# Loading the gate-up weights of a mixture of experts in pairs of chunks, ahead of the down weights

## The reference, cut to what matters

```
for each of 32 experts e:                      # every token has 4 of them
    h = xb @ w_gu[e] + b_gu[e]                 # w_gu[e]: 1024 x 2048, 8 MB
    h_gate, h_up = split(h, 2)                 # clipped at 7
    act = h_gate * sigmoid(1.702 * h_gate) * (h_up + 1)
    y[tokens of e] += gate * (act @ w_down[e] + b_down[e])   # w_down[e]: 1024 x 1024, 4 MB
```

## Time and profile before

| what | us |
|---|---|
| median of 3 runs (2065.43 to 2068.64) | 2066.38 |
| the profiled execution: time | 2069.82 |
| its span, first to last instruction | 2068.0 |
| PE busy | 1988.8 |
| DVE busy | 894.7 |
| ACT busy | 686.3 |
| first expert's first gate-up matmul | 1150.93 |

### The profile page before, as it was taken

One profiled execution on the slowest core, in us unless ns is written; L12 is line 12 of the kernel. 1 busy time (PEld: TensorE's weight loads), 2 busy tenths in 40 slices (PEclk: granted clock), 3 DMA queues, 4 the chain that ended last, 5 costly groups with the idle time before them and its releaser, 6 DMA issues.

```text
span 2068.0 us, 29157 instructions
## 1 busy us (share of the span) xinstructions
PE 1988.8 (96%) x12306; PEld 1384.8 (67%) x12306; DVE 894.7 (43%) x1070; ACT 686.3 (33%) x941; POOL 39.1 (2%) x30
## 2 busy tenths in 40 slices
PE   8999999999999998999999999999999999999997
PEld 8998768999999886999998544444343333433343
DVE  6766666676666787666645211111111111111112
ACT  5545475545555566444444111111001000101011
POOL 0700000000000000000000000000000000000000
PEclk9999999999999998999999899999999999999999
DMA  9663607556556442555296999999999999999997
GB/s 317 196 223 131 235 1 257 191 184 200 170 190 208 166 162 74 173 202 184 95 333 247 372 426 427 427 428 428 429 428 429 428 429 428 429 428 429 428 429 318
DMA packets 165568, 603.88 MB, mean 292 GB/s; under 512 B 9324, under 2 KB 102464, under 8 KB 140564
## 3 DMA queue, kind: packets, MB, share of 16 engines
q1 hardware_dynamic: 165328, 602.79, 74.9%
q10 hardware_dynamic: 164, 0.04, 0.0%
HBM read 601.71 MB, written 1.09 MB: 291 GB/s over the span
## 4 chain that ended last, share of the span: by engine, by line
PE 69%; DMA 22%; DVE 4%; ACT 3%; issue 1%; SPq 0%; DVEq 0%; ACTq 0%
PE ps L1832 13%; PE ps L1834 13%; PE ps L1833 13%; PE ps L2412 12%; DMA sb_w_free<-in_moe_w_gate_up 7%; PE ps L2436 5%; DMA sb_raw<-in_moe_w_down 5%; DMA sb_raw<-in_moe_w_gate_up 3%; DMA sb_w_free<-in_moe_w_down 3%; PE ps L2382 2%; DMA sb_nat_more<-in_moe_w_gate_up 2%; DMA sb_late_raw<-in_moe_w_down 2%; ACT sb_w_hi L669 1%; PE ps L2444 1%; PE ps L2393 1%; DVE sb_w_lo L1112 1%
## 5 line engine op out<-in xcount | busy, mean ns | idle before, releaser
L1112 DVE TENSOR_TENSOR sb_w_lo<-sb_raw,sb_w_hi 128x2048 fp32r<-128x2048 f32 x175 | 403.0, 2312 | 233.8 <-ACT sb_w_hi L669 233.3
L669 ACT ACTIVATE sb_w_hi<-sb_raw 128x2048 fp32r<-128x2048 f32 x179 | 340.5, 1912 | 167.9 <-PE ps L1834 147.6
L1832 PE MATMUL ps<-sb_xT_hi,sb_w_hi 128*128 128x256 f32 x1344 | 373.2, 278 | 0.0
L1833 PE MATMUL ps<-sb_xT_lo,sb_w_hi 128*128 128x256 f32 x1344 | 372.7, 277 | 0.0
L1834 PE MATMUL ps<-sb_xT_hi,sb_w_lo 128*128 128x256 f32 x1344 | 372.6, 277 | 0.0
L1833 PEld LDWEIGHTS ps<-sb_xT_lo,sb_w_hi 128*128 128x128 f32 x1344 | 252.8, 188 | 1.5
L1832 PEld LDWEIGHTS ps<-sb_xT_hi,sb_w_hi 128*128 128x128 f32 x1344 | 252.3, 188 | 1.7 <-DVE sb_w_lo L1112 0.2
L1834 PEld LDWEIGHTS ps<-sb_xT_hi,sb_w_lo 128*128 128x128 f32 x1344 | 253.2, 188 | 0.0
L1027 ACT ACTIVATE sb_h_rows<-ps 128x512 f32<-128x512 f32 x32 | 19.2, 599 | 424.1 <-PE ps L2412 424.1
L1707 DVE COPY sb_h_rows<-ps 128x512 f32<-128x512 f32 x31 | 21.4, 692 | 317.2 <-PE ps L2412 317.2
L1834 PE MATMUL ps<-sb_w_hi,sb_a_lo 128*128 128x512 f32 x352 | 138.5, 393 | 0.0
(11 more groups left out here) (320 smaller groups left out, 2678.8 us busy)
## 6 DMA issues: line engine op xcount, KB each, us to landing
sb_raw<-in_moe_w_gate_up SPq DMA_DIRECT2D x49, 2048.0 KB, 34.5
sb_w_free<-in_moe_w_gate_up SPq DMA_DIRECT2D x46, 2048.0 KB, 34.5
sb_w_free<-in_moe_w_down SPq DMA_DIRECT2D x24, 2048.0 KB, 33.9
sb_raw<-in_ffn_w_up SPq DMA_DIRECT2D x44, 1024.0 KB, 5.3
sb_raw<-in_ffn_w_down SPq DMA_DIRECT2D x44, 1024.0 KB, 5.0
sb_raw<-in_moe_w_down SPq DMA_DIRECT2D x22, 2048.0 KB, 33.9
sb_raw<-in_ffn_w_gate SPq DMA_DIRECT2D x43, 1024.0 KB, 5.4
sb_late_raw<-in_moe_w_gate_up SPq DMA_DIRECT2D x17, 2048.0 KB, 35.2
```

Of the source, the lines that this page charges most:

```text
L669: sc.activation(w_hi[:, c % CUT, :], raw[:, c % RAW, :], ACT.Copy).then_inc(hi_made, 1)
L1112: ve.tensor_tensor(w_lo[:, c % CUT, :], raw[:, c % RAW, :], w_hi[:, c % CUT, :].bitcast(F32), ALU.subtract).then_inc(lo_made, 1)
L1832: pe.matmul(o, l_hi, r_hi, start=start, stop=False)
L1833: pe.matmul(o, l_hi, r_lo, start=False, stop=False)
```

## The change

Places 4 and 5 become adjacent in SBUF: `raw` and `w_free` are now parts of one tensor, `ring_space`. The order of a step's chunks becomes gate-up 0, gate-up 1, down 0, down 1, gate-up 2, gate-up 3, in the loads and on PE, and so for all steps. In steps 5 to 29 (gate-up of experts 6 to 30) two gate-up chunks whose places are adjacent (0 and 1, 4 and 5, 6 and 7) are one DMA of 4 MB, in which a partition gets 32 KB in one piece. It waits until both places are free and signals the semaphore of the first place; PE waits for it before the first chunk of the pair and for nothing before the second. A pair that would lie in places 2 and 3 stays two DMAs (`alone`). Since a partition now holds four neighbouring rows of a pair, a chunk that is loaded alone reads 16 KB of each 32 KB, and `gather` takes every fourth column of x where it took every second. The numbers of the kept down chunks and of the chunk after which outputs are read move by one.

```
-        raw = sb("raw", [P, RAW, CH])
         cuts = ExitStack()
+        sb("below_cuts", [P, RAW, CH], stack=cuts)
...
-        w_free = sb("w_free", [P, 2 * CUT, CH])
+        ring_space = sb("ring_space", [P, RAW + 2 * CUT, CH])
+        raw, w_free = ring_space[:, 0:RAW, :], ring_space[:, RAW:RAW + 2 * CUT, :]
...
+        slot_pairs = {k: ring_space[:, 4 * k:4 * k + 4, :].rearrange("p a n -> p (a n)") for k in range(3)}
+        pair_at = {0: 0, 4: 1, 6: 2}
...
+        def alone(t, first):
+
+            start, end = step_t(LOOP_S[0]) if first else 4, step_t(N_E - 2)
+            return t % 2 == 0 or t % RING == 3 or t < start or t >= end or (t - 4) % EXPERT_C in (2, 3)
...
-                    src = a["moe_w_gate_up_2"][0][bass.ds(e, 1), 256 * j:256 * (j + 1), :].rearrange(
-                        "e (p k) n -> p (e k) n", p=P)
+                    src = a["moe_w_gate_up_2"][0][bass.ds(e, 1), 512 * (j // 2):512 * (j // 2 + 1), :].rearrange(
+                        "e (p q k) n -> p q (e k) n", p=P, q=2)[:, j % 2]
...
+            def gate_up_pair(e, j, t, laps=0):
+
+                if alone(t + 1, isinstance(laps, int)):
+                    expert_chunk("gate_up", e, j, t, laps)
+                    expert_chunk("gate_up", e, j + 1, t + 1, laps)
+                    return
+                src = a["moe_w_gate_up_2"][0][bass.ds(e, 1), 256 * j:256 * (j + 2), :].rearrange("e (p k) n -> p (e k n)", p=P)
+                sp.wait_ge(chunk_used, used_no(t + 1, laps) - RING)
+                sp.dma_start(slot_pairs[pair_at[t % RING]], src).then_inc(slot_loaded[t % RING], 16)
...
             def step_loads(e, s, laps=0, first=0):
 
+                t = step_t(s)
                 if first == 0:
-                    expert_chunk("gate_up", e + 1, 0, step_t(s), laps)
+                    gate_up_pair(e + 1, 0, t, laps)
                     for j in range(2):
-                        if step_t(s) + 1 + j not in KEPT_T:
-                            expert_chunk("down", e, j, step_t(s) + 1 + j, laps)
-                for j in range(max(1, first), 4):
-                    expert_chunk("gate_up", e + 1, j, step_t(s) + 2 + j, laps)
+                        if t + 2 + j not in KEPT_T:
+                            expert_chunk("down", e, j, t + 2 + j, laps)
+                gate_up_pair(e + 1, 2, t + 4, laps)
...
-                    j, odd = divmod(k0 + m, 2)
-                    w = slice(2 * j * P + odd, 2 * (j + 1) * P, 2)
+                    j, row = divmod(k0 + m, 4)
+                    w = slice(4 * j * P + row, 4 * (j + 1) * P, 4)
...
-                pe.wait_ge(slot_loaded[t % RING], loaded_no(t, laps, r))
+                if alone(t, isinstance(r, int)):
+                    pe.wait_ge(slot_loaded[t % RING], loaded_no(t, laps, r))
...
-                gate_up_rows(left, t, 0, laps, r)
+                for j in range(2):
+                    gate_up_rows(left, t + j, j, laps, r)
                 pe.wait_ge(m_g_made, e + 1)
                 turn_picks(base4, s)
                 pe.wait_ge(m_act_made, e + 1)
                 for j in range(2):
-                    down_rows(t + 1 + j, j, laps, r)
+                    down_rows(t + 2 + j, j, laps, r)
...
-                for j in range(1, 4):
+                for j in range(2, 4):
                     gate_up_rows(left, t + 2 + j, j, laps, r)
```

More of the change, by code:

```diff
@@ L94 @@
 LOOPS = (N_E - 8) // 4
-KEPT_T = (4 + EXPERT_C * KEPT_E + 1, 4 + EXPERT_C * KEPT_E + 2)
+KEPT_T = (4 + EXPERT_C * KEPT_E + 2, 4 + EXPERT_C * KEPT_E + 3)
 REL_W = 256
@@ L327, in build, with loaded_no @@
         used_no = lambda t, laps: MOE_C0 + t + 1 + RING * laps
[L329 to L333, removed]
+        def alone(t, first):
+            start, end = step_t(LOOP_S[0]) if first else 4, step_t(N_E - 2)
+            return t % 2 == 0 or t % RING == 3 or t < start or t >= end or (t - 4) % EXPERT_C in (2, 3)
+        def loaded_no(t, quads, r):
+            own = lambda first: [k for k in range(t % RING, ROUND_C, RING) if alone(k, first) and k not in KEPT_T]
+            upto = lambda first: len([k for k in own(first) if k <= t])
+            in_quad = 16 * (3 if t % 2 == 0 or t % RING == 3 else 1) * quads
+            if isinstance(r, int):
+                return 16 * upto(True) + in_quad
+            return 16 * (upto(False) + len(own(True)) - len(own(False))) + in_quad + 16 * len(own(False)) * r
         g_kv, g_in, g_out = (lambda i: 8 * i), (lambda i: 8 * i + 1), (lambda i: 8 * i + 6)
@@ L570, in _ @@
             sp.wait_ge(chunk_used, MOE_C0 - 1)
-            expert_chunk("down", 0, 0, 5)
+            expert_chunk("gate_up", 1, 1, 5)
             sp.wait_ge(chunk_used, MOE_C0)
-            expert_chunk("down", 0, 1, 6)
-            expert_chunk("gate_up", 1, 1, 7)
+            expert_chunk("down", 0, 0, 6)
+            expert_chunk("down", 0, 1, 7)
             sp.wait_ge(logits_done, 1)
@@ L1052, in step @@
                 turned_picks(e, s % 2)
-                outputs(e, s % 2, t + 2, laps)
+                outputs(e, s % 2, t + 3, laps)
             def last_two(r):
@@ L2581, in first_round @@
                     for s in LOOP_S:
-                        step(4 * it, it, s, 3 * it, 0)
+                        step(4 * it, it, s, it, 0)
                 step(0, 0, N_E - 3, 0, 0)
@@ L2589, in another_round @@
                     for s in range(8):
-                        step(N_E * r + 8 * it, QUADS * r + 2 * it, s, 6 * it, r)
+                        step(N_E * r + 8 * it, QUADS * r + 2 * it, s, 2 * it, r)
                 for s in range(N_E - 8, N_E - 2):
```

## The result

The change makes the kernel **slower by 0.5%**: 2077.20 us (median of 6 runs, 2074.02 to 2080.38) against 2066.43 us (6 runs), ratio 1.005 with a 95% interval of 1.0037 to 1.0063. I had forecast 2066.3 us within 2062.8 to 2071.5 us; both the value and the range missed.

A forecast was written before the change was run, and what follows sets the result against it. The weight stream was taken to set the pace from about 1430 us (29.37 us a step), PE before that and in the tail. +3.4 - 3.5 = -0.1 us gave 2066.3 us from 2066.38 us, range 2062.8 to 2071.5 us.

The forecast's parts named there:

- part 4: Order on PE and gather's stride of 4: at worst 0.24 us a step, hidden, so nothing at the end.
- the hole: PE's wait before a paired block in the DMA-paced part: one of about 2.9 us a step in place of three short ones.
- part 3: The ring: a pair waits for its later place, issued some 4 us later; queue 34.5 us deep, never empty, priced at nothing.
- three signs of a wrong forecast: Load wait on the chain behind 2000 us; step over 29.4 us; DMA share below 1.0 between 1210 and 2000 us.
- Part 1: Tail: two blocks instead of one behind the landing of the last pair, chunks 176 and 177, +3.4 us.
- Part 2: Weight stream before chunk 177: 36 paired DMAs with 8 packets fewer per engine, at 12 ns a packet, -3.5 us.
- The line through my two points: Packet price from two stretches, 611.7 ns at 16 KB and 182.9 ns at 4657 B: 36.6 ps a byte, 12 ns a packet.
- clock rival: TensorE's clock falls in the hole before the pair 176/177, costing 1.75 to 6.75 us; 2068.0 to 2073 us, chance 0.19.
- slow-stream rival: Weight stream slower with 32 KB pieces or half-read strides, 1% costing 7 us; 2071 us and more, chance 0.07.

The follow-up runs named there:

- e7: Kernel before with the turns of the gate and up rows done as plain matmuls by the identity instead of transposes; a single execution took 2100.32 us.
- e8: Kernel before with gather at a stride of 4 only in the first step and steps 0 to 12, steps 5 to 12 written out; ratio 1.0071, stage 926.2 us.
- e11: Kernel before with steps 5 to 12 written out on PE instead of looped, gather at a stride of 2 throughout; ratio 1.0020, stage 919.4 us.
- e1: Changed kernel, pairs kept, with gather reading x at a stride of 2 as before the change; ratio 1.0005 to the kernel before, stage 920.4 us.
- e10: Kernel before with each partition's two gate-up rows taken from two HBM places, two 8 KB packets instead of one of 16 KB; a single execution took 2076.82 us.
- e3: Changed kernel with every gate-up chunk loaded alone from consecutive rows and gather at stride 2, leaving only the new order; ratio 1.0000 to the kernel before.
- e4: Changed kernel without pairs, each gate-up chunk reading 16 KB of each 32 KB, gather at stride 4; ratio 1.0041 to the kernel before, stage 924.4 us.
- e2: Kernel before with gather reading x at a stride of 4; ratio 1.0029, stage (first gate-up matmul to span end) 924.4 us against 917.1 us.

## Why the prediction was wrong

**The step that failed** is part 4, "`turn_rows` does so already", with its "At worst 0.24 us a step; hidden in the hole, and before 1430 us it only eats the spare of later". Both halves fell. The price was 1.85 us a step (3.93 against 2.08 us), because I took it from transposes, and e7 shows that the same operand costs a matmul 328 ns. And it wasn't hidden: before 1430 us the stream itself lives on the places that PE frees. When PE's step gets longer there, places come free later, the queue runs empty, and the lost stream time isn't made up, because from the takeover on the stream is the bound. The window 1100 to 1430 us moved 134.92 MB before and 130.63 MB after, 4.29 MB or 10.0 us at 428 GB/s, in which the experts' start 0.45 us later is contained; e8 less e11 shows that the loss is in the early steps. The same mistake is in part 3: the depth of 34.5 us is that of the stream-paced part. I named the condition, "if the queue did run dry, each late microsecond would move the end by one", and it came true. Two of the three signs of a wrong forecast came true as well: a wait for a load behind 2000 us (2000.79 us), and a DMA share below 1.0 (0.99 and 0.98 between 1200 and 1400 us); the step stayed below 29.4 us.

**Part 1**, +3.4 us behind the last landing, was right: +3.5 us.

**Part 2** was right in its mechanism: the data packets of 1430 to 1990 us went from 14647 to 10978 (12349 - 1371), a quarter fewer, and the rate to 430 GB/s, as forecast:

```profile
DMA packets 12349, 240.98 MB, mean 430 GB/s; under 512 B 1371, under 2 KB 1371, under 8 KB 1371
```

The size was off: 9.7 ns instead of 12 ns a packet, 36 x 8 x 9.7 ns = -2.8 us instead of -3.5 us; in e1 the landing came 2.9 us earlier. An estimate by the cycle count of the Trainium skill, "DMA: Bandwidth & Descriptors", section "Why small descriptors are slow", would have been 3.5 ns and -1.0 us; the measured 9.7 ns of e10 decides. (The line through my two points, without rounding the slope, gives 12.5 ns; that changes nothing.)

**Part 3**: the order alone costs nothing (e3), the half-read pieces nothing (e4). That a pair is issued later isn't free where PE paces and the queue is short already: over 1300 to 1400 us e2 has 423 GB/s, e4 416 GB/s and the change, with pairs, 406 GB/s, where the kernel before has 428 GB/s. With pairs and a stride of 2 (e1) that stretch has 429 GB/s. So the pairs widen gaps that the stride opens, and open none by themselves.

**The sum, as it should have been**: +3.5 behind the landing, -2.8 by packets, +9.3 us of stream lost early makes +10.0 us. The 9.3 us are what is left of the landing's +6.5 us once the 2.8 us are taken out, and the 9.8 us that the change lacks in the first 280 us count them another way. Of the 9.3 us, 7.3 are the stride's by the stages of e2 and e4 (6.7 by e8 less e11); the other 2.0 us fit the 2.4 us of stream that the change lacks against e4, from 1300 us on. All of these come from single executions.

**The rivals.** The clock rival is real as a mechanism, the first time that the hole appears (e1), but no hole before a pair slowed this change: there the mean clock of 1300 to 2000 us is 1.00. One dip lies ahead of that: after 0.83 us without work at 1281.4 us the granted clock is 0.57 from 1282 to 1286 us, and a block takes 5.11 instead of 3.65 us. e2 has such a dip too (0.83 over 1270 to 1280 us), e8 has none and loses its 6.7 us all the same; so the dip isn't needed for the loss, but up to 1.5 us of it may be the dip's, and no run separates them. That the hole before a pair stayed at 0.84 and 0.90 us is luck as far as my forecast goes: the long loads that I had priced at nothing filled it. Of the slow-stream rival only the sign came true; the stream was slower by running dry early, not by its pieces. None of my rivals had the queue running empty under a slower PE, and that is what the missing 9.3 us were.

## What to carry to other kernels

When a bound changes hands during a stage, a slack has to be read for each part: work on the engine that leads early moves the end even if the other resource leads later, as long as the second one is fed by what the first frees; so take queue depth and slack from the part in which the cost falls. Take the price of an operand pattern from the same kind of operation: a transpose and a 32-bit matmul on the same operand cost differently. Merging two loads saved the cost of a packet here, but puts all work on the merged data behind one landing; look at what stands behind the last one.

## What the runs showed of the hardware that I had not expected

A stationary load of 128x128 32-bit elements for a matmul takes 191 ns at a stride of 1, 196 ns at 2 and 328 ns at 4; for a transpose it takes 209 ns at 4. A packet costs 9.7 ns beyond its bytes between 8 and 16 KB (e10), and 9.4 ns between 16 and 32 KB (the changed kernel). A stream that reads 16 KB of each 32 KB is as fast as one that reads all (29.37 us a step, e4). After a single hole of 2.7 us in otherwise dense work the granted clock fell to 0.50, and two blocks that take 7.09 us took 10.10 us; of eleven such holes in e1 nine were followed by slower blocks. In the changed kernel the clock fell once after only 0.83 us without work.
